# Gate projections of a two-layer decoder trunk as matmuls 512 columns wide, with a changed order on VectorE and ScalarE

## The reference

```
h = rms_norm(x, norm1_g) * (1 + sc1) + sh1
z, xbc, dt, q, k, v, gate_s, gate_a = split(h @ w_in)           # z is 2048 wide
xs, B, C = split(silu(causal_conv4(xbc)))                       # 2048, 4*128, 4*128
y = ssd_chunked(xs, softplus(dt), A, B, C) + d_skip * xs        # 4 groups of 8 heads, chunks of 128 tokens
y = y * silu(z)                                                 # the gate of this case
y = y * rsqrt(mean(y*y over each group of 512) + eps) * norm_g
y_ssm = y @ w_ssm_out
y_att = diff_attention(q, k, v) @ w_attn_out
x = x + g1 * ((sigmoid(gate_s) * y_ssm + sigmoid(gate_a) * y_att) @ w_out)
h = rms_norm(x, norm2_g) * (1 + sc2) + sh2
x = x + g2 * (relu(h @ w_ff1)**2 @ w_ff2)
```

## Time and profile before

| | |
|---|---|
| median of 3 runs | 2317.44 us (2317.39 to 2318.23) |
| the profiled execution | 2317.45 us, its span 2315.4 us |
| granted TensorE clock over the span | 0.995 |
| busy TensorE, weight load | 2274.4 us (98%), 1903.4 us (82%) |
| busy VectorE | 1372.5 us (59%) |
| busy ScalarE | 1030.0 us (44%) |
| busy GpSimd | 1105.3 us (48%) |
| DMA | 267.18 MB, mean 115 GB/s |

### The profile page before, as it was taken

One profiled execution on the slowest core, in us unless ns is written; L12 is line 12 of the kernel. 1 busy time (PEld: TensorE's weight loads), 2 busy tenths in 40 slices (PEclk: granted clock), 3 DMA queues, 4 the chain that ended last, 5 costly groups with the idle time before them and its releaser, 6 DMA issues.

```text
span 2315.4 us, 32138 instructions
## 1 busy us (share of the span) xinstructions
PE 2274.4 (98%) x11808; PEld 1903.4 (82%) x11808; DVE 1372.5 (59%) x2079; ACT 1030.0 (44%) x1882; POOL 1105.3 (48%) x825
## 2 busy tenths in 40 slices
PE   7999999999999999999989999999999999999997
PEld 6888998888878888888878889988888788888886
DVE  7678767556653787877757777612566436422224
ACT  2566653266653342222335666533566434332331
POOL 1466555433444454444435555554334444644542
PEclk9999999999999999999999999999999999999998
DMA  6333336422224345545422433222222232332231
GB/s 253 116 96 117 107 105 191 155 74 73 74 74 164 109 141 209 184 180 193 152 98 89 125 109 101 88 96 91 74 73 74 73 118 91 109 100 93 99 100 46
DMA packets 94124, 267.18 MB, mean 115 GB/s; under 512 B 8528, under 2 KB 35536, under 8 KB 88592
## 3 DMA queue, kind: packets, MB, share of 16 engines
q1 hardware_dynamic: 73776, 237.73, 30.2%
q10 hardware_dynamic: 20192, 27.40, 3.9%
HBM read 260.77 MB, written 4.33 MB: 114 GB/s over the span
## 4 chain that ended last, share of the span: by engine, by line
PE 60%; issue 18%; POOL 8%; POOLq 8%; DVE 2%; DVEq 1%; PEld 1%; DMA 1%; ACTq 1%; ACT 0%; SPq 0%; PEldq 0%
PE gemm L552 13%; PE gemm L554 13%; PE gemm L553 13%; POOL w_lo L1900 8%; POOLq L1902 8%; PE gemm L575 3%; PE gemm L576 3%; PE gemm L577 3%; PE aux L617 3%; PE aux L796 2%; PE aux L726 2%; PE aux L834 2%; PE aux L740 1%; PE aux L735 1%; DMA ada_pe<-stream 1%
## 5 line engine op out<-in xcount | busy, mean ns | idle before, releaser
L1900 POOL TENSOR_TENSOR w_lo<-raw,w_hi 128x512 fp32r<-128x512 f32 x704 | 973.4, 1404 | 1068.8 <-ACT w_hi L949 1060.4
L949 ACT ACTIVATE w_hi<-raw 128x1024 fp32r<-128x1024 f32 x352 | 370.8, 1058 | 677.4 <-PE gemm L554 607.2
L552 PE MATMUL gemm<-h_hi,w_hi 128*128 128x512 f32 x1472 | 589.8, 401 | 0.8 <-issue 0.8
L554 PE MATMUL gemm<-h_hi,w_lo 128*128 128x512 f32 x1472 | 575.3, 391 | 0.0
L553 PE MATMUL gemm<-h_lo,w_hi 128*128 128x512 f32 x1472 | 574.1, 390 | 0.0
L554 PEld LDWEIGHTS gemm<-h_hi,w_lo 128*128 128x128 f32 x1472 | 276.7, 188 | 59.9
L552 PEld LDWEIGHTS gemm<-h_hi,w_hi 128*128 128x128 f32 x1472 | 277.4, 188 | 58.1 <-issue 4.6
L553 PEld LDWEIGHTS gemm<-h_lo,w_hi 128*128 128x128 f32 x1472 | 277.4, 188 | 56.1 <-issue 1.9
L552 PE MATMUL gemm<-op_hi,w_hi 128*128 128x512 f32 x608 | 238.6, 392 | 0.2
L554 PE MATMUL gemm<-op_hi,w_lo 128*128 128x512 f32 x608 | 236.8, 389 | 0.0
L553 PE MATMUL gemm<-op_lo,w_hi 128*128 128x512 f32 x608 | 236.6, 389 | 0.0
(11 more groups left out here) (210 smaller groups left out, 3387.6 us busy)
## 6 DMA issues: line engine op xcount, KB each, us to landing
raw<-stream SPq DMA_DIRECT2D x336, 512.0 KB
ada_late<-stream SPq DMA_DIRECT2D x30, 1024.0 KB, 4.9
seg<-decay_rows ACTq DMA_DIRECT2D x64, 256.0 KB, 3.3
ada_early<-stream ACTq DMA_DIRECT2D x40, 256.0 KB, 4.2
raw<-stream SPq DMA_DIRECT2D x32, 256.0 KB
ada_first<-stream SPq DMA_DIRECT2D x5, 1024.0 KB, 20.6
x<-xT SPq DMA_DIRECT2D x2, 2048.0 KB, 10.3
ada_pe<-stream SPq DMA_DIRECT2D x3, 1024.0 KB, 14.2
```

What stands on the lines that cost most here:

```text
L552: mm(o, w_hi[:, slot, k, cols], hi[:, k, :], start=k == 0, stop=False)
L554: last = mm(o, w_lo[:, slot, k, cols], hi[:, k, :], start=False, stop=k == KB - 1)
L949: A(w_hi[:, slot, ks], raw[:, slot, ks], ACT.Copy).then_inc(hi_ready, 1)
L1900: gp.tensor_tensor(w_lo[:, slot, ks], raw[:, slot, ks], w_hi[:, slot, ks].bitcast(F32), ALU.subtract)
```

## The change

A z unit now holds 512 outputs by 512 inputs. Two units together (an even and an odd one, "late") make a group, and all four banks take the group, one bank for 128 tokens. `gate_tokens` does 6 matmuls of 512 columns for a part, in place of 12 of 256. The four banks are complete at the last four parts of the odd unit, one after another; three of them tell it by a new semaphore `z_done`. The first z unit has another order of its parts, and its second half is opened at its third part. Part (0, 2) of each even unit waits for `bank_free[1]`. Each half of a unit is loaded by two DMAs, which interleave the rows of two units of the stream.

ScalarE's tanh_z reads a bank once; the copy to `zh` is gone. VectorE's gate_y reads z from PSUM, and its factor one half stands in the second operation. The gate of a token block runs in the tick of the part that completes it (`Z_AT`): for group 0 one in tick 22 and three in tick 23, for group 1 two in tick 27 and two in tick 28, for group 2 four in tick 33, for group 3 four in tick 37. Before, there was one each in ticks 21, 22, 24, 25, 26, 27, 29, 30, 32 to 39.

VectorE does y_low and y_normed ahead of the mask, and ScalarE take_y ahead of the decay.

```diff
+PART_TICK = [_tick for _tick in range(T_FIRST, T_END) for _ in range(fill_of(_tick))]
+FIRST_GATE = ((0, 0), (0, 1), (1, 0), (1, 1), (0, 2), (0, 3), (1, 2), (1, 3))
+Z_AT = {}
+for _n in range(N_Z // 2 * TB):
+    Z_AT.setdefault(PART_TICK[KB * (U_Z + 2 * (_n // TB) + 1) + TB + _n % TB], []).append(divmod(_n, TB))
...
-        zt = place("zt", [P, 2, UW], F32, r_z)
-        zh = place("zh", [P, 2, UW], F32, r_z + T2)
+        zt = place("zt", [P, 2, S], F32, r_z)
...
+                elif U_Z <= n < U_O:
+                    rows = slice((n - U_Z) % 2 * TB + 2 * half, (n - U_Z) % 2 * TB + 2 * half + 2)
+                    for a in range(2):
+                        sp.dma_start(raw[:, slot, TB * half + a:TB * half + TB:2],
+                                     unit_of(l, place_of(n - (n - U_Z) % 2 + a))[:, rows]).then_inc(raw_in[slot][half], 16)
...
+            def gate_tokens(l, n, part):
+                slot, late = n % 2, (n - U_Z) % 2
+                half, t = FIRST_GATE[part] if n == U_Z else divmod(part, TB)
+                o = gb[t][:]
+                toks = slice(t * P, (t + 1) * P)
+                if not late and (half, t) == (0, 2):
+                    pe.wait_ge(bank_free[1], freed_at(l, n + 1) - 2)
+                for r in range(2 * half, 2 * half + 2):
+                    k = TB * late + r
+                    hi = w_hi[:, slot, 2 * r:2 * r + 2, :].rearrange("p a n -> p (a n)")
+                    lo = w_lo[:, slot, 2 * r:2 * r + 2, :].rearrange("p a n -> p (a n)")
+                    mm(o, h_hi[:, k, toks], hi, start=k == 0, stop=False)
+                    mm(o, h_lo[:, k, toks], hi, start=False, stop=False)
+                    last = mm(o, h_hi[:, k, toks], lo, start=False, stop=k == KB - 1)
+                if t == TB - 1:
+                    last.then_inc(gemm_done, 1)
+                elif late and half:
+                    last.then_inc(S_["z_done"], 1)
...
-                    if k % (KB // 2) == 0:
+                    if n == U_Z:
+                        if k % 2 == 0 and k < TB:
+                            open_half(l, n, k // 2)
+                    elif k % (KB // 2) == 0:
                         open_half(l, n, k // (KB // 2))
-                    if U_Z <= n < U_O or n == U_Q + 2 or (U_AT <= n < U_AO and AT_UNITS[n - U_AT][0] == "v"):
+                    if U_Z <= n < U_O:
+                        gate_tokens(l, n, k)
+                    elif n == U_Q + 2 or (U_AT <= n < U_AO and AT_UNITS[n - U_AT][0] == "v"):
                         unit_tokens(n % 2, k)
...
-                def tanh_z(n, j):
-                    act.wait_ge(gemm_done, done_at(l, n))
-
-                    act.wait_ge(S_["z_used"], mid_at(l, "z_used", 2 * (n - U_Z) + j) + Z_CREDIT)
-                    src = gb[2 * (n % 2) + j][:].rearrange("p (t n) -> p t n", t=2)
-                    A(zt[:], src, ACT.Tanh, scale=0.5)
-                    A(zh[:], src, ACT.Copy, scale=0.5).then_inc(bank_free[n % 2], 1)
-                    act.drain().then_inc(S_["z_act"], 1)
+                def tanh_z(g, t):
+                    if t < TB - 1:
+                        act.wait_ge(S_["z_done"], mid_at(l, "z_done", 3 * g + t) + 1)
+                    else:
+                        act.wait_ge(gemm_done, done_at(l, U_Z + 2 * g + 1))
+
+                    act.wait_ge(S_["z_used"], mid_at(l, "z_used", TB * g + t) - 1 + Z_CREDIT)
+                    A(zt[:, t % 2], gb[t][:], ACT.Tanh, scale=0.5).then_inc(S_["z_act"], 1)
...
+                    for _, key in EXTRA.get(tick - 1, ()):
+                        if key[0] == "y":
+                            take_y(*key[1:])
                     if 0 <= tick + 1 < T_POST:
                         decay(tick + 1)
...
-                def gate_y(n, j):
-
-                    g, u = divmod(n - U_Z, 2)
-                    dve.wait_ge(S_["z_act"], mid_at(l, "z_act", 2 * (n - U_Z) + j) + 1)
-                    STT(zt[:], zt[:], 1.0, zh[:], ALU.add, ALU.mult)
+                def gate_y(g, t):
+
+                    dve.wait_ge(S_["z_act"], mid_at(l, "z_act", TB * g + t) + 1)
+                    STT(zt[:, t % 2], zt[:, t % 2], 1.0, gb[t][:], ALU.add, ALU.mult).then_inc(bank_free[t // 2], 1)
                     settle()
-                    yv = y_tok[:, g, 2 * j:2 * j + 2, u * UW:(u + 1) * UW]
-                    TT(yv, yv, zt[:], ALU.mult)
+                    yv = y_tok[:, g, t, :]
+                    STT(yv, zt[:, t % 2], 0.5, yv, ALU.mult, ALU.mult)
                     dve.drain().then_inc(S_["z_used"], 1)
...
-                    if tick == 2:
-                        wait_freed(l, ("cd",))
-                    if 0 <= tick + 1 < T_POST:
-                        masked(tick + 1)
                     for _, key in EXTRA.get(tick - 1, ()):
                         if key[0] == "y":
                             y_low(*key[1:])
                     for _, key in EXTRA.get(tick, ()):
                         if key[0] == "y":
                             y_normed(*key[1:])
+                    if tick == 2:
+                        wait_freed(l, ("cd",))
+                    if 0 <= tick + 1 < T_POST:
+                        masked(tick + 1)
...
-                    for j in range(2):
-                        for n in since(tick, U_Z, U_O, 1 + j):
-                            gate_y(n, j)
+                    for g, t in Z_AT.get(tick, ()):
+                        gate_y(g, t)
```

More of the change, by code:

```diff
@@ L170 @@
     ("mid", 1, {"seed": 24, "taps": 24, "tanh": 24, "silu": 24, "decay": 32, "m": 32, "m_used": 16, "xdt": 4, "xd": 4, "dx": 4, "state": 12,
[L171 removed]
+                "z_done": 12, "z_act": 16, "z_used": 16, "y_sq": 4, "y_ms": 4, "y_rs": 4, "yn": 16, "y_hi": 16, "y_lo": 16,
                 "swap": 16, "rope": 16, "v": 4, "mx": 32, "e": 32, "p": 32, "pt": 32, "o_sq": 8, "o_ms": 8, "o_rs": 8,
@@ L375, in build @@
         LO_CREDIT, DONE_CREDIT, BANK_CREDIT, AUX_CREDIT, LAYER_CREDIT = 0, 4, 2, 1, 1
-        SILU_CREDIT, U_CREDIT, ROPE_CREDIT, Z_CREDIT, OUT_CREDIT, X_CREDIT = 4, 4, 2, 1, 2, KB
+        SILU_CREDIT, U_CREDIT, ROPE_CREDIT, Z_CREDIT, OUT_CREDIT, X_CREDIT = 4, 4, 2, 2, 2, KB
         GT_CREDIT = 2
@@ L1166, in act_program @@
                             act.wait_ge(x_saved, 16)
-                        if key[0] != "cb":
+                        if key[0] not in ("cb", "y"):
                             takes[key[0]](*key[1:])
@@ L1178, in act_program @@
                         exp_of_dt()
-                    for j in range(2):
-                        for n in since(tick, U_Z, U_O, 1 + j):
-                            tanh_z(n, j)
+                    for g, t in Z_AT.get(tick, ()):
+                        tanh_z(g, t)
                     for g in range(GROUPS):
@@ L1776, in dve_program @@
                         dve.wait_ge(gemm_done, done_at(l, U_AO + u))
-                        STT(zt[:].rearrange("p a n -> p (a n)"), gate_a[:, 2 * u + j, :], 1.0, gb[c][:], ALU.add, ALU.mult)\
+                        STT(zt[:, 0], gate_a[:, 2 * u + j, :], 1.0, gb[c][:], ALU.add, ALU.mult)\
                             .then_inc(bank_free[u % 2], 1)
                         settle()
-                        TT(mix[:, 2 * u + j, :], mix[:, 2 * u + j, :], zt[:].rearrange("p a n -> p (a n)"), ALU.add)
+                        TT(mix[:, 2 * u + j, :], mix[:, 2 * u + j, :], zt[:, 0], ALU.add)
                         dve.drain().then_inc(S_["mixed"], 1)
```

## The result

The changed kernel takes 2324.0 us, median of 11 runs (2321.89 to 2325.44); the kernel before, beside it on the same chip, 2317.82 (11 runs, 2317.39 to 2318.23). The ratio is 1.0026 [1.0018, 1.0033]: 6.2 us slower, outside the range of the prediction. The profiled execution took 2324.00 with a span of 2322.1, against 2317.45 and 2315.4.

What follows compares the result with a forecast made beforehand. The prediction took TensorE's matmul pace as the bound, VectorE next. From 2317.45 us, -9.5 (matmuls) + 3.0 (tick 19) + 2.4 (ticks 27 to 30) + 1.0 (ticks 33, 34) + 2.7 (ticks 37, 38) gave 2317.0; range 2308.5 to 2322.

Steps and rivals of the forecast that it cites:

- second rival: VectorE becomes the bound of the y stage through clustered gates in ticks 28 to 30, 34 and 38: 2323.6 us, chance 18%.
- Every sign that was named for the forecast being right: Gate steps 0.228 us; taps wait 1.3 to 1.7 in tick 19; normed-block waits over 3.1, longest in tick 38; bank wait there.
- those against it: No TensorE idle time from 280 to 305 us; first-to-third normed block chain under 13 us; matmul steps over 0.235.
- The matmuls: Gate stream: 768 pairs of 256-column matmuls become 768 single 512-column ones, saving 9.5 us (bounds 0 to 9.5).
- Tick 19: First z group: TensorE newly waits for the convolution's last taps, 1.35 and 1.7 us in the two layers: +3.0 us.
- Ticks 27 to 30: Group 0's y stage: two gates each in ticks 27 and 28 delay normed blocks: +2.4 us (-1.8 to +4.6).
- last rival: The change's banks work otherwise: a wait for bank_free[1] at every group; chance small, counted within the other cases.
- Tick 34: Four gates in tick 33 make tick 34's normed block late by 0.5 us: +1.0 in both layers (0 to 4).
- Ticks 37 and 38: First layer: four gates behind six DMA issues, bank wait 1.4, block wait 2.7: +2.7 us (-1.4 to +4); second at most 0.2.
- The order of VectorE and ScalarE: Mask behind the normed block gives little; take_y ahead of the decay costs 0, at most 0.3 us a tick.
- Loads: Each half of a unit comes by two DMAs of smaller pieces: cost 0, at most 0.5 us.
- ScalarE's copies: ScalarE loses 32 copies, which lay beside matmuls: nothing on the path.

Runs made afterwards that it cites:

- pair of kernels: The changed kernel and the kernel before, both without the second operation of each gate (e2 and e11): 2309.31 and 2314.69 us.
- e5: Changed kernel with the last two gates of group 3 at ticks 38 and 39, and the taps ahead of the mask in tick 18: 2314.55 us.
- e4: Changed kernel with VectorE's taps ahead of the mask in tick 18 alone: 2319.22 us, ten runs in two groups of five.
- e1: Changed kernel with the old order on VectorE (mask ahead of y_low and y_normed) and ScalarE (take_y behind the decay): 2323.38 us.
- e3: Changed kernel with the last two gates of group 3 moved from tick 37 to ticks 38 and 39: 2317.96 us.
- e2: Changed kernel without the second operation of each gate, so y is not multiplied by silu(z): 2309.31 us.
- e7: Changed kernel with the first ten pieces of `early`, DMA issues and VectorE's part alike, one tick later: 2318.29 us.
- e8: Changed kernel with the edits of e5, e6 and e7 together: 2317.44 us.
- e11: Kernel before the change without the second operation of each gate, so y is not multiplied by silu(z): 2314.69 us.
- e6: e5 with the y stage of group 0 one tick later (28 to 31 in place of 27 to 30): 2319.61 us.
- e9: e5 with the second operations of group 1's gates moved to ticks 29 to 31, on four buffers of tanh in place of two: 2313.52 us.
- e10: e9 and e7 together: 2311.94 us, the fastest that does the whole computation.

## Why the prediction was wrong

The forecast was 2317.0; what happened is its second rival, VectorE as the bound of the y stage, priced at 2323.6 with 18%. Every sign that was named for the forecast being right came true, and none of those against it: the places of the waits were right, the time was not, and the signs tested the places alone. Point by point:

- **The matmuls**, -9.5 forecast: -8.1 by the steps, -7.1 by the pair of kernels. The wide stream steps 0.229, not 0.2276, and the first matmul of a run takes 0.32 from start to start. Steps stayed under 0.235, and the bound below (0) was far off. The formula of the Trainium skill that was weighed (TensorE: Matmul & The Clock Gate, "Back-to-back issue gap") would have given 1.9, an estimate. The section gives it for a single matmul on its own, and some 131 ns a matmul of 512 columns for a stream in which each has its weight load; the 0.229 us of the trace agree with neither, and the runs side with the trace.
- **Tick 19**, +3.0 forecast: 1.3 + 1.6 = 2.9, and e5 recovers 3.4 by taking it away. Right, in place and size. (By medians e4 gives 4.8, but they mix its two groups of times; e5's 3.4 is the better one.)
- **Ticks 27 to 30**, +2.4 forecast: start to start, waits of 1.23, 0.56, 1.01 and 0.22 make 3.0 a layer, where before had 1.2 (its two waits of the earlier trace rows, 0.40 and 0.48 idle, are 0.57 and 0.65 from start to start): +1.8 a layer, +3.6. The chain of VectorE was forecast at 7.42 and 7.28 us between normed blocks; it took 288.54 - 281.07 = 7.47 and 297.42 - 288.54 = 8.88. The 1.6 missing are the block and the mask that GpSimd's low part disturbed. I had priced the added gates at 1.57 each, undisturbed, and let the rest of the chain keep the durations of before. Once ticks 27 and 28 hold two gates each, the chain shifts, and other operations stand beside the low part. The bank wait in tick 29 is not in the sum. It is the mechanism of the last rival, a wait for `bank_free[1]`: the second pair of gates frees those banks, the last one at 293.26 + 0.69 = 293.95, and TensorE restarts at 294.01. I had looked at it in tick 24 alone, where there was slack.
- **Tick 34**, +1.0 forecast: 0.52 in each layer. Right; the four gates took VectorE 7.8 us where I had 8.0.
- **Ticks 37 and 38**, +2.7 forecast, is the step that failed: it is off by 2.5, the largest of all, and with it at +2.7 the sum below would lie within the range. Bank wait forecast 1.4, measured 0.90; block wait forecast 2.7, measured 354.37 - 350.65 = 3.72, less a normal step 3.5. Together 4.4 in place of 1.6, +2.8, as forecast. But TensorE, having stood for 3.3 us, then ran 3.4 us at the 1.2 GHz level, which cost 1.6; and the second layer, forecast at no more than 0.2, gave 0.74. That is 2.8 + 1.6 + 0.7 = +5.2. I took the price of a wait to be its length.
- **The order of VectorE and ScalarE**, forecast as small: nothing that can be told (e1). **Loads**: no wait for them appeared. **ScalarE's copies**, nothing on the path: no run tests them alone, and no row contradicts it.
- **The sum**: -8.1 + 2.9 + 3.6 + 1.0 + 5.2 = +4.6. Between the layers the stretch at the lower clock was 13.7 us long where before had 10.2. It costs about 1.1 us more: from the last transposes of the first layer to the first ones of the second takes 1036.5 us in the changed kernel, and 1035.3 in e3, whose code is the same there and whose stretch is short. Both lengths occur among the kernels run, e2 to e5, e7, e8 and e11 having the short one and e1, e6, e9 and e10 the long one. I take it for scatter and not for an effect of the change; with one trace of each kernel that isn't shown. With it the sum is +5.7, against 6.2 by the medians and 6.5 between the two profiled executions. Some 0.4 of the rest are the four restarts of the wide stream behind a wait, whose first step is 0.33 (294.01 to 294.34) and not 0.23.
- **The condition of the rival.** I said that it decides when a gate costs 2.3 and the root comes at 282.7. Neither was so: VectorE's normed block started at 281.07, before even my 281.5, and the four gates of ticks 27 and 28 took 1.6 each. The rival had the right place and a price near the true one, for reasons that were half wrong. VectorE had no slack for four gates in two ticks even with each at its undisturbed price. That many operations of the gates of before ran disturbed was no evidence for or against it.

The duration of the gate's two operations on VectorE in the changed kernel (ns min/median/max):

```profile
L1621 DVE SCALAR_TENSOR_TENSOR zt<-zt,gemm x32: 673/687/689, 251.4 to 1496.8; 128x512 f32<-128x512 f32 x32
L1624 DVE SCALAR_TENSOR_TENSOR y_tok<-zt,y_tok x32: 691/694/1678, 252.2 to 1497.6; 128x512 f32<-128x512 f32 x32
```

What remains open: what decides whether the clock falls after a wait; what parts e4's two groups of times; and some 2 us of e2, which gained 14.7 where the rows give 12.8: 8.3 for the normed blocks, 0.8 for the bank of tick 29, 0.6 less in the row of L562 (the bank of tick 38), 0.4 less in the row of the taps, 1.6 for the clock and 1.1 for the stretch between the layers, 10.2 us long in it.

## What to carry to other kernels

A saving spread over a stream can be lost at the few places where the other engine's work became clustered: work out, for every deadline, that engine's chain from one deadline to the next, and allow for the disturbed duration on whichever operations GpSimd's work may fall beside, not on those that it met before. A long wait of TensorE in a busy stream (3.3 us here) is priced at its length and, with some chance, half as much again for the clock. When work is regrouped, its due times and those of whatever shares the engine (here `early` and its DMA issues) have to be set anew: moving the taps, two late gates, four second operations and `early` turned 6 us of loss into 6 of gain.

## What the hardware showed beyond the forecast

- The granted clock fell to 0.50 for 3.4 us, beginning some 1.2 us after TensorE had resumed from a wait of 3.3. In e4 the same wait was followed by 1.00 throughout. In e1 it happened twice, once behind a wait of only 1.65 us in tick 29 (windows ahead of and behind that restart at 299.5). Its second layer has a wait of 1.82 at the same place and no fall, and neither have the waits of 1.6 to 1.8 in e6. So the length of the wait alone doesn't decide it:

```profile
296.00:299.60 3.60, 1.95 (x12) 1.15 (x11) 3.38 (x5) 1.34 (x4) 1.31 (x1) 1.00 0.38 106
299.60:303.00 3.40, 3.40 (x11) 2.83 (x12) 3.05 (x6) 0.69 (x1) 0.00 (x0) 0.50 0.22 76
```

- The first operation of the gate, with a PSUM operand, took 673 to 689 ns in all 32 cases, though 13 of them lay beside a GpSimd operation. The second, all in SBUF, took over 800 in 11 of 32, up to 1678, each of them beside GpSimd. The Trainium skill (SBUF — State Buffer, "SBUF: two separate sides") says that a VectorE operation with two SBUF inputs and a GpSimd one that reads SBUF take a port pair in turns, each holding it for a whole instruction; the rows of tick 28 above, 1.53 and 1.76 beside two GpSimd operations of 2.96 together, agree with it.
